# Banded attention with five key tiles: two turned tiles to ScalarE and three to VectorE, instead of one and four

## The chip, the core and the metric

One core of a Trainium2 chip runs the whole program. The metric is the device time in microseconds of one launch. The engines that matter here are TensorE (PE in the profile, its weight loads PEld), VectorE (DVE) and ScalarE (ACT); they run their own instruction streams and meet at semaphores.

## What is computed

A trunk of two layers over 2048 tokens of width 1024, in float32. Layer 0 runs a differential attention and a sliding-window attention; layer 1 projects its input and runs a chunked attention of 16 heads of 64, in which every chunk of 64 tokens attends to itself and the 8 chunks before it. Only the last is touched:

```
def one_chunk(args):
    qi, c = args
    start = c * CHUNK
    kb = lax.dynamic_slice_in_dim(kp, start, C_BAND, axis=2)
    vb = lax.dynamic_slice_in_dim(vp, start, C_BAND, axis=2)
    s = jnp.einsum('bhqd,bhkd->bhqk', qi, kb, preferred_element_type=jnp.float32) * ATTN_SCALE + bias
    s = jnp.where((start + koff) >= 0, s, -jnp.inf)
    p = jax.nn.softmax(s, axis=-1)
    return jnp.einsum('bhqk,bhkd->bhqd', p.astype(vb.dtype), vb)
```

## The kernel before

The program is a row of stages: project, diff_attn, band_attn (prefix b_), output, project, band_attn (prefix c_), output. The stages run one behind the other. band_attn is written once and used twice: with `back` = 1 (b_, a step is at most two key tiles wide) and with `back` = 4 (c_, up to five).

A step s of band_attn handles one tile of 128 queries (i = s % 16) of one pair of heads (hp = s // 16). Its `width(s)` is the number of key tiles of 128: 1, 2, 3, 4 in the first steps of a pair of heads, then 5 in the other twelve. With 16 heads there are 8 pairs and 128 steps, 96 of them five tiles wide, called full here. A step goes through these hands:

- qk(s), TensorE, line 1438: logits of both heads, into two accumulators of PSUM that every step uses again, so it waits for both maxima of step s-1.
- maximum(s, half), VectorE, line 1519: adds the bias, takes the row's extreme and writes to SBUF, one instruction and an accumulator read for each head.
- exponential(s, half), ScalarE, line 1550, in place, with the sum of the row.
- transposes(s), TensorE, line 1459: turns the 64-row halves of `prob` (chunk by chunk, `a`, tile by tile, `t`) into PSUM. The upper 64 rows and the lower 64 rows are worked off in pairs: while the upper half writes into its bank of `turned`, the lower one writes into another bank. Tiles from MAIN on, the far ones, go to the bank `turned_far`, which both halves use: the lower half does its far tiles first, the upper half last, and between them stands the semaphore `far_begun`.
- main_leaves(s), VectorE, line 1527: copies the tiles up to MAIN from `turned` to `prob_t` in SBUF.
- far_leaves(s), ScalarE, line 1563: copies the far tile from `turned_far`.
- pv(s), TensorE, line 1478: multiplies with the values; waits for both copies of step s.
- output_leaves, ScalarE, line 1557, every fourth step: copies the finished block out of PSUM.

The order on each engine is written out by hand. TensorE: qk(s), transposes(s-1), pv(s-2). VectorE: maximum(s, 0), maximum(s, 1), main_leaves(s-1). ScalarE: exponential(s, 0), exponential(s, 1), far_leaves(s-1), and every fourth step output_leaves. transposes(s) waits for the exponentials of s and, since `turned` and `turned_far` exist once, for both copies of step s-1. GpSimd only prepares biases and the output weights beside it, and SyncE issues the loads and stores.

Of the kernel before, what the change touches and what calls it, by code (L numbers as in the profile page):

```python
# [26 lines left out]
P = 128  # L27
# [3 lines left out]
BLK = 512  # L31
NBLK = SEQ // BLK
TPB = BLK // P
HD = 64
# [1201 lines left out]
def band_attn(nc, before, name, keep, scr, heads, back, q_row, k_row, group, v_dram, skew, o_row, sinks, w_dram, w_loaded, w_hi, w_lo, post, share, ready=None, ssq=None, rms=None):  # L1236
# [4 lines left out]
    with ExitStack() as ctx:  # L1241
# [4 lines left out]
        sums = post.sums  # L1246
        WIDE = (back + 1) * P
        SPARE = 1 if sinks else 0
        MAIN = 4
        bias = st.sb("bias", [P, 4, WIDE]) if ready is None else ready.bias  # L1250
        prob = st.sb("prob", [P, 4, WIDE + SPARE])
        prob_t = st.sb("prob_t", [P, 2, back + 1, 2, P])
# [4 lines left out]
        END = BLK + NEAR  # L1257
        turned = st.ps("turned", [P, 2, BLK])
        turned_far = st.ps("turned_far", [P, BLK])
        o_ps = st.ps("o", [P, BLK])  # L1260
        HALVES = 2
        HALF = SEQ // HALVES
# [8 lines left out]
        pair_turned, far_begun, main_copied, far_copied = (st.sem(x) for x in ("pair_turned", "far_begun", "main_copied", "far_copied"))  # L1271
# [12 lines left out]
        def k_set(hp):  # L1284
            return hp % 2 if group == 1 else 2 * hp // group

        def loads(hp):
            return (hp - own_from) // 2 + 1

        def width(s):  # L1290
            return min(s % TILES, back) + 1

        def full(s):
            return min(width(s), MAIN)

        fars = [sum(width(e) > MAIN for e in range(s)) for s in range(PAIRS + 1)]

# [115 lines left out]
        @block.tensor  # L1413
        def _(pe):
            def qk(s):
                hp, i = divmod(s, TILES)
                b, kb, w = hp % 2, k_set(hp), width(s)
                if ready is not None:
                    if s == 0:
                        pe.wait_ge(ready.loaded, ready.LOADED)  # L1420
                elif hp == 0:
                    for n, (lo, hi) in enumerate(FIRST):
                        if i == lo // P:
                            pe.wait_ge(first_loaded[n], 16 * (LOADS + 1))
                if hp >= own_from and i % (TILES // HALVES) == 0:
                    pe.wait_ge(pair_loaded[b][i // (TILES // HALVES)], 16 * LOADS * loads(hp))
                if ready is not None and hp == 2 and i == 0:
                    pe.wait_ge(ready.keys_loaded, ready.KEYS_LOADED)
                if s >= 1:
                    pe.wait_ge(max_done, 2 * s)  # L1430
                cuts = [(END - w * P, BLK, i - w + 1)] if w > 2 else []
                near = min(w, 2)
                cuts.append((END - near * P, END, i - near + 1))
                for lo, hi, tile in cuts:
                    for n, (x, y) in enumerate(((0, 0), (0, 1), (1, 0))):
                        for half in range(2):
                            rows = slice(half * HD, (half + 1) * HD)
                            last = nc.tensor.matmul(logits[half][:, lo:hi], q_sb[b][x][rows, i * P:(i + 1) * P],  # L1438
                                                    k_sb[kb][y][rows, tile * P:tile * P + hi - lo], start=n == 0, stop=n == 2)
                last.then_inc(qk_done, 1)  # L1440

            def transposes(s):
                if s >= 1:
                    pe.wait_ge(main_copied, s)
                    if fars[s] > fars[s - 1]:
                        pe.wait_ge(far_copied, fars[s])
                main = [[(a, t) for t in range(full(s))] for a in range(2)]
                far = [[(a, t) for t in range(MAIN, width(s))] for a in range(2)]
                upper, lower = main[0] + main[1] + far[0] + far[1], far[0] + far[1] + main[0] + main[1]
                pe.wait_ge(exp_done, 2 * s + (2 if far[0] else 1))  # L1450
                for n in range(len(upper)):
                    if n == full(s):
                        pe.wait_ge(exp_done, 2 * s + 2)
                    if far[0] and n == 2 * MAIN:
                        pe.wait_ge(far_begun, fars[s + 1])
                    for part, (a, t) in enumerate((upper[n], lower[n])):
                        rows = slice(part * HD, (part + 1) * HD)
                        to = turned[:, part, (2 * t + a) * HD:(2 * t + a + 1) * HD] if t < MAIN else turned_far[:, (2 * part + a) * HD:(2 * part + a + 1) * HD]
                        last = nc.tensor.transpose(to, prob[rows, (2 * s + a) % 4, t * P:(t + 1) * P], keep["ident"][rows, rows])  # L1459
                    if far[0] and n == 1:  # L1460
                        last.then_inc(far_begun, 1)
                last.then_inc(pair_turned, 1)

            def pv(s):
                hp, i = divmod(s, TILES)
                pe.wait_ge(main_copied, s + 1)
                if fars[s + 1] > fars[s]:
                    pe.wait_ge(far_copied, fars[s + 1])
                if s % GROUP == 0 and s >= GROUP:
                    pe.wait_ge(o_done, s // GROUP)  # L1470
                if ready is None and hp >= own_from and i % (TILES // HALVES) == 0:
                    pe.wait_ge(v_loaded[hp % 2][i // (TILES // HALVES)], 16 * loads(hp))
                at = s % GROUP * P
                w = width(s)
                for t in range(w):
                    for half in range(2):
                        v = v_sb[:, hp % 2, half, i - w + 1 + t, :] if ready is None else v_sb[:, k_set(hp), i - w + 1 + t, :]
                        last = nc.tensor.matmul(o_ps[half * HD:(half + 1) * HD, at:at + P], v,  # L1478
                                                prob_t[:, s % 2, t, half, :], start=t == 0, stop=t == w - 1)
                last.then_inc(pv_done, 1)  # L1480

            if sinks:
                pe.wait_ge(zero_set, len(logits))
            for s in range(PAIRS + 2):
                if s < PAIRS:
                    qk(s)
                if 1 <= s <= PAIRS:
                    transposes(s - 1)
                if s >= 2:
                    pv(s - 2)  # L1490
# [52 lines left out]
        @block.scalar  # L1543
        def _(act):
            def exponential(s, half):
                hp, i = divmod(s, TILES)
                j = (2 * s + half) % 4
                act.wait_ge(max_done, 2 * s + half + 1)
                p = prob[:, j, 0:width(s) * P + SPARE]
                nc.scalar.activation(p, p, ACT.Exp, bias=neg_max[:, j:j + 1], scale=-1.0,  # L1550
                                     accum_out=sums[:, 2 * hp + half, i:i + 1]).then_inc(exp_done, 1)

            def output_leaves(n):
                act.wait_ge(pv_done, (n + 1) * GROUP)
                if n >= 2:
                    act.wait_ge(stored[n % 2], 16 * (n // 2))
                nc.scalar.activation(o_out[:, n % 2, :], o_ps[:, :], ACT.Copy).then_inc(o_done, 1)

            def far_leaves(s):
                act.wait_ge(pair_turned, s + 1)  # L1560
                if s >= 2:
                    act.wait_ge(pv_done, s - 1)
                nc.scalar.copy(prob_t[:, s % 2, MAIN, :, :].rearrange("p a (r q) -> p r a q", r=2),
                               turned_far[:, 0:2 * P].rearrange("p (r a q) -> p r a q", r=2, a=2)).then_inc(far_copied, 1)

            if ready is None:
                for n in range(len(FIRST)):
                    first_piece(act, n, 1)
            for s in range(PAIRS + 2):
                if s < PAIRS:  # L1570
                    exponential(s, 0)
                    exponential(s, 1)
                if 1 <= s <= PAIRS and width(s - 1) > MAIN:
                    far_leaves(s - 1)
                if s == PAIRS and ssq is not None:
                    act.wait_ge(mean_done, 1)
                    nc.scalar.activation(root[:, :, :], mean[:, :, :], ACT.Sqrt).then_inc(root_done, 1)
                if s >= 2 and (s - 2) % GROUP == GROUP - 1:
                    output_leaves((s - 2) // GROUP)
# [248 lines left out]
```

## Time and profile before

| | us |
|---|---|
| median of 3 runs | 2651.3 (2649.97 to 2653.81) |
| the profiled execution | 2649.35 |
| its span, first to last instruction | 2647.5 |
| TensorE busy in the span | 2384.7 (90%) |
| VectorE busy | 1473.0 (56%) |
| ScalarE busy | 1161.6 (44%) |
| GpSimd busy | 1132.2 (43%) |

The page of the profile gives busy shares over the whole span, which holds seven stages with different limits; the stage at hand takes about 390 us of it, from 2046 to 2440 us. It has to be read from the timeline of its own steps. In the rows below, times are microseconds from the span's start; in brackets stands how long the engine had been idle and what ended most of it. The timeline merges neighbouring instructions of a kind into one row with a count. The ends of matmuls are modelled.

### The profile page before, as it was taken

The page shows a single profiled execution, that of the slowest core. Times are in us where ns is not written, and L with a number is a line of the kernel's source. Part 1 is how long each engine was busy: PE and PEld are TensorE (multiplying, and loading weights), DVE is VectorE, ACT ScalarE, POOL GpSimd, SP SyncE. Part 2 cuts the span into 40 slices and gives each one's busy share as a digit, 9 for nine tenths or more (in the row PEclk, how much of TensorE's full clock was granted, in tenths as well). Part 3 has the DMA queues.
Part 4 walks back from the last instruction along what each step waited for, and adds up shares of the span by engine and source line. Part 5 has one row for each costly group of instructions (what it writes and reads, how often), then busy time and mean ns, then how long its engine had stood idle before and what let it go on. Part 6 is the DMA issues. An engine that isn't in the chain of part 4 may idle for free. (4 is left out here: it accounts for less than half of the span.)

```text
span 2647.5 us, 44254 instructions
## 1 busy us (share of the span) xinstructions
PE 2384.7 (90%) x16760; PEld 1996.6 (75%) x16760; DVE 1473.0 (56%) x2823; ACT 1161.6 (44%) x2484; POOL 1132.2 (43%) x892
## 2 busy tenths in 40 slices
PE   2999979996899998989959999799997899998998
PEld 2877868875778876668848888688886778887887
DVE  4344445334887795755634422544323778887565
ACT  5333343333777775722133333433332666665211
POOL 5887878771000002311058887888874201100000
PEclk7999989998999999989979999899999999999999
DMA  3455434457563133565534443434433453453352
GB/s 103 151 191 183 140 118 149 149 172 153 118 140 92 45 120 89 167 216 207 199 109 154 164 130 100 155 125 170 131 100 108 167 192 122 145 173 113 138 212 80
DMA packets 220882, 376.63 MB, mean 142 GB/s; under 512 B 54996, under 2 KB 109440, under 8 KB 219648
## 3 DMA queue, kind: packets, MB, share of 16 engines
q1 hardware_dynamic: 199280, 297.78, 35.2%
q0 software_dynamic: 18992, 72.36, 9.2%
q10 hardware_dynamic: 2400, 3.67, 0.5%
q8 instruction: 135, 2.21, 0.3%
q14 instruction: 75, 0.61, 0.1%
HBM read 236.33 MB, written 142.90 MB: 143 GB/s over the span
## 5 line engine op out<-in xcount | busy, mean ns | idle before, releaser
L808 PE MATMUL p_acc<-p_a_hi,p_w_hi 128*128 128x512 f32 x1624 | 643.4, 396 | 37.0 <-DVE p_a_lo L593 33.5
L808 PE MATMUL p_acc<-p_a_hi,p_w_lo 128*128 128x512 f32 x1624 | 636.8, 392 | 0.0
L808 PE MATMUL p_acc<-p_a_lo,p_w_hi 128*128 128x512 f32 x1624 | 636.1, 392 | 0.0
L236 POOL TENSOR_TENSOR p_w_lo<-p_w_raw,p_w_hi 128x512 fp32r<-128x512 f32 x252 | 350.6, 1401 | 121.0 <-ACT p_w_hi L474 120.5
L808 PEld LDWEIGHTS p_acc<-p_a_hi,p_w_hi 128*128 128x128 f32 x1624 | 307.6, 189 | 106.1 <-DVE p_a_lo L593 34.6
L808 PEld LDWEIGHTS p_acc<-p_a_hi,p_w_lo 128*128 128x128 f32 x1624 | 307.1, 189 | 65.5
L808 PEld LDWEIGHTS p_acc<-p_a_lo,p_w_hi 128*128 128x128 f32 x1624 | 307.7, 189 | 62.3
L474 ACT ACTIVATE p_w_hi<-p_w_raw 128x512 fp32r<-128x512 f32 x252 | 156.7, 623 | 268.6 <-POOL p_w_raw L254 110.3
L1550 ACT ACTIVATE c_prob<-c_prob,c_neg_max 128x640 f32<-128x640 f32 (+4 forms) x256 | 193.2, 755 | 142.4 <-DVE c_neg_max L1519 141.9
L667 DVE SCALAR_TENSOR_TENSOR p_lo_out<-p_full_out,p_hi_out 128x512 fp32r<-128x512 f32 x116 | 125.0, 1078 | 208.1 <-ACT p_hi_out L488 208.1
L1519 DVE CUSTOM_DVE_ANT_0 c_prob<-c_logits,c_bias 128x640 f32<-128x640 f32 (+4 forms) x256 | 179.5, 738 | 81.0 <-PE c_logits L1438 61.7
L1744 PE MATMUL o_acc<-w_out_hi,o_m_hi 128*128 128x512 f32 x512 | 203.7, 398 | 4.8 <-DVE o_m_lo L1696 4.8
L1744 PE MATMUL o_acc<-w_out_hi,o_m_lo 128*128 128x512 f32 x512 | 201.0, 393 | 0.0
L1744 PE MATMUL o_acc<-w_out_lo,o_m_hi 128*128 128x512 f32 x512 | 200.9, 392 | 0.0
L1103 ACT ACTIVATE a_prob<-a_prob,a_neg_max 128x128 f32<-128x128 f32 (+15 forms) x128 | 153.5, 1199 | 47.2 <-DVE a_neg_max L1063 46.4
L1438 PE MATMUL c_logits<-share 64*128 64x256 f32 (+2 forms) x1440 | 138.2, 322 | 33.2 <-DVE c_neg_max L1519 16.1
L696 DVE COPY p_full_out<-p_acc 128x512 f32<-128x512 f32 x58 | 40.1, 691 | 216.3 <-PE p_acc L808 216.2
L1438 PEld LDWEIGHTS c_logits<-share 64*128 64x128 f32 x1440 | 111.9, 188 | 58.1 <-DVE c_neg_max L1519 27.9
L1478 PE MATMUL c_o<-c_prob_t,c_v 128*64 128x128 f32 x2240 | 151.6, 279 | 1.6 <-issue 1.6
L236 POOL TENSOR_TENSOR p_w_lo<-ready_w,p_w_hi 128x512 fp32r<-128x512 f32 x96 | 132.3, 1388 | 36.8 <-ACT p_w_hi L474 36.4
L1527 DVE COPY c_prob_t<-c_turned 128x1024 f32<-128x1024 f32 (+3 forms) x128 | 143.3, 1120 | 6.1 <-PE c_turned L1459 6.1
L474 ACT ACTIVATE p_w_hi<-p_t 128x512 fp32r<-128x512 f32 x58 | 36.6, 632 | 239.9 <-issue 122.5
(192 smaller groups left out, 4338.0 us busy)
## 6 DMA issues: line engine op xcount, KB each, us to landing
scr_qh<-p_hi_out SPq DMA_DIRECT2D x116, 256.0 KB, 2.4
scr_ql<-p_lo_out SPq DMA_DIRECT2D x116, 256.0 KB, 2.6
p_w_raw<-in_w_in_even POOLq DMA_DIRECT2D x26, 1024.0 KB, 7.6
scr_gt<-p_hi_out SPq DMA_DIRECT2D x128, 128.0 KB, 2.0
ready_w<-in_w_in_odd POOLq DMA_DIRECT2D x16, 1024.0 KB, 7.7
p_w_raw<-in_w_in_odd POOLq DMA_DIRECT2D x16, 1024.0 KB, 7.5
share<-scr_qh SPq DMA_DIRECT2D x28, 512.0 KB, 9.3
share<-scr_ql SPq DMA_DIRECT2D x28, 512.0 KB, 10.4
```

The lines of the kernel that those rows point to most:

```text
L236: nc.gpsimd.tensor_tensor(w_lo[:, k, :, :], w_source(e, k), w_hi[:, k, :, :].bitcast(F32), ALU.subtract).then_inc(w_made, 1)
L474: nc.scalar.activation(w_hi[:, k, :, :], w_source(e, k), ACT.Copy).then_inc(w_cast, 1)
L667: nc.vector.scalar_tensor_tensor(out=lo_out[:, buf, :], in0=full_out[:, buf, :], scalar=factor, in1=hi_out[:, buf, :].bitcast(F32), op0=AL ...
L696: nc.vector.tensor_copy(full_out[:, n % 2, :], x[:, :]).then_inc(taken, 1)
L808: last = nc.tensor.matmul(bank[:, :], wt[:, k, c, :], at[:, k, c, :], start=starts and step == 0, stop=step == 3 * HK - 1, skip_group_chec ...
L1103: nc.scalar.activation(p, p, ACT.Exp, bias=neg_max[:, j:j + 1], scale=-1.0, accum_out=row_sum[:, g % 2, m:m + 1]).then_inc(exp_done, 1)
L1438: last = nc.tensor.matmul(logits[half][:, lo:hi], q_sb[b][x][rows, i * P:(i + 1) * P], k_sb[kb][y][rows, tile * P:tile * P + hi - lo], sta ...
L1478: last = nc.tensor.matmul(o_ps[half * HD:(half + 1) * HD, at:at + P], v, prob_t[:, s % 2, t, half, :], start=t == 0, stop=t == w - 1)
L1519: nc.vector.tensor_tensor_reduce(out=prob[:, j, 0:n + SPARE], in0=logits[half][:, END - n:END + SPARE], in1=bias[:, b, WIDE - n:WIDE + SPARE],
L1527: nc.vector.tensor_copy(prob_t[:, s % 2, 0:n, :, :].rearrange("p t a (r q) -> p r (t a) q", r=2), turned[:, :, 0:n * P].rearrange("p r (x ...
L1550: nc.scalar.activation(p, p, ACT.Exp, bias=neg_max[:, j:j + 1], scale=-1.0, accum_out=sums[:, 2 * hp + half, i:i + 1]).then_inc(exp_done, 1)
L1744: last = nc.tensor.matmul(acc[u % 4][:, :], mt[:, t % 2, c, :], wt[:, c, half * BLK:(half + 1) * BLK], start=step == 0, stop=step == 3 * K ...
```

## The change

MAIN goes from 4 to 3. VectorE copies the first three key tiles of a step and ScalarE the tiles from the fourth on: two in a five-tile step and one in a four-tile step, where before it had none. In `turned_far` the lower half's tiles now begin at the middle of the bank (FAR), and ScalarE's copy takes both. The lower half turns all its far tiles first, four transposes in a full step where there were two, and signals `far_begun` behind the last of them, the 8th transpose of the step instead of the 4th; the upper half waits for it ahead of its own far tiles, which are now its last four instead of its last two: ahead of the 13th transpose instead of the 17th. The b_ stage, with at most two tiles, issues the same instructions as before.

```diff
--- before.py
+++ after.py
@@ -1246,7 +1246,7 @@
         sums = post.sums
         WIDE = (back + 1) * P
         SPARE = 1 if sinks else 0
-        MAIN = 4
+        MAIN = 3
         bias = st.sb("bias", [P, 4, WIDE]) if ready is None else ready.bias
         prob = st.sb("prob", [P, 4, WIDE + SPARE])
         prob_t = st.sb("prob_t", [P, 2, back + 1, 2, P])
@@ -1257,6 +1257,7 @@
         END = BLK + NEAR
         turned = st.ps("turned", [P, 2, BLK])
         turned_far = st.ps("turned_far", [P, BLK])
+        FAR = BLK // 2
         o_ps = st.ps("o", [P, BLK])
         HALVES = 2
         HALF = SEQ // HALVES
@@ -1455,9 +1456,9 @@
                         pe.wait_ge(far_begun, fars[s + 1])
                     for part, (a, t) in enumerate((upper[n], lower[n])):
                         rows = slice(part * HD, (part + 1) * HD)
-                        to = turned[:, part, (2 * t + a) * HD:(2 * t + a + 1) * HD] if t < MAIN else turned_far[:, (2 * part + a) * HD:(2 * part + a + 1) * HD]
+                        to = turned[:, part, (2 * t + a) * HD:(2 * t + a + 1) * HD] if t < MAIN else turned_far[:, FAR * part + (2 * (t - MAIN) + a) * HD:FAR * part + (2 * (t - MAIN) + a + 1) * HD]
                         last = nc.tensor.transpose(to, prob[rows, (2 * s + a) % 4, t * P:(t + 1) * P], keep["ident"][rows, rows])
-                    if far[0] and n == 1:
+                    if far[0] and n == 2 * len(far[0]) - 1:
                         last.then_inc(far_begun, 1)
                 last.then_inc(pair_turned, 1)
 
@@ -1560,8 +1561,9 @@
                 act.wait_ge(pair_turned, s + 1)
                 if s >= 2:
                     act.wait_ge(pv_done, s - 1)
-                nc.scalar.copy(prob_t[:, s % 2, MAIN, :, :].rearrange("p a (r q) -> p r a q", r=2),
-                               turned_far[:, 0:2 * P].rearrange("p (r a q) -> p r a q", r=2, a=2)).then_inc(far_copied, 1)
+                n = width(s) - MAIN
+                nc.scalar.copy(prob_t[:, s % 2, MAIN:MAIN + n, :, :].rearrange("p t a (r q) -> p r (t a) q", r=2),
+                               turned_far[:, :].rearrange("p (r x q) -> p r x q", r=2, q=HD)[:, :, 0:2 * n, :]).then_inc(far_copied, 1)
 
             if ready is None:
                 for n in range(len(FIRST)):
```

## Rows read from the trace of the kernel before

**Rows 1.** Stretches of c_: length, busy PE, PEld, DVE, ACT, POOL, clock, DMA share, GB/s

```profile
2046.00:2092.00 46.00, 36.66 (x546) 31.99 (x548) 29.92 (x65) 24.66 (x63) 9.03 (x8) 0.82 0.68 259
2092.00:2440.00 348.00, 322.03 (x5381) 282.02 (x5377) 285.21 (x577) 222.80 (x578) 31.61 (x31) 1.00 0.44 140
```

**Rows 2.** Timeline of TensorE over two full steps: start, duration (us), line, operation, count

```profile
2078.11 1.16 PE L1438 MATMUL c_logits<-share 64*128 64x384 f32 x12
2079.13 0.24 PE L1459 MATMUL c_turned<-keep_ident,c_prob 64*128 64x64 f32 x1
...
2079.89 1.31 PE L1478 MATMUL c_o<-c_prob_t,c_v 128*64 128x128 f32 x20
2081.13 1.16 PE L1438 MATMUL c_logits<-share 64*128 64x384 f32 x12
2082.37 0.24 PE L1459 MATMUL c_turned<-keep_ident,c_prob 64*128 64x64 f32 x1
...
2082.49 0.22 PE L1459 MATMUL c_turned_far<-keep_ident,c_prob 64*128 64x64 f32 x1
...
2082.89 0.22 PE L1459 MATMUL c_turned_far<-keep_ident,c_prob 64*128 64x64 f32 x1
...
2084.38 1.16 PE L1438 MATMUL c_logits<-share 64*128 64x384 f32 x12
```

**Rows 3.** Timeline of VectorE, same steps

```profile
2079.41 0.82 DVE L1519 CUSTOM_DVE_ANT_0 c_prob<-c_logits,c_bias 128x640 f32<-128x640 f32 x1 [0.53 <-PE c_logits L1438]
...
2080.91 1.22 DVE L1527 COPY c_prob_t<-c_turned 128x1024 f32<-128x1024 f32 x1
2082.44 0.82 DVE L1519 CUSTOM_DVE_ANT_0 c_prob<-c_logits,c_bias 128x640 f32<-128x640 f32 x1 [0.31 <-PE c_logits L1438]
```

**Rows 4.** Timeline of ScalarE, same steps

```profile
2081.11 0.82 ACT L1550 ACTIVATE c_prob<-c_prob,c_neg_max 128x640 f32<-128x640 f32 x1
...
2081.93 0.35 ACT L1563 COPY c_prob_t<-c_turned_far 128x256 f32<-128x256 f32 x1
```

**Rows 5.** Waits in the steady stretch: who waited for whom, us in total, times, longest

```profile
PEld c_turned L1459 <- DVE c_prob_t L1527: 18.2, 50, 1.4
...
PE c_turned L1459 <- ACT c_prob_t L1563: 7.7, 21, 1.2
```

**Rows 6.** Groups by shape in one head pair: count, busy us, mean ns, idle before

```profile
L1550 ACT ACTIVATE c_prob<-c_prob,c_neg_max 128x640 f32<-128x640 f32 x24 | 19.7, 822 | 12.4 <-DVE c_neg_max L1519 12.4
...
L1527 DVE COPY c_prob_t<-c_turned 128x1024 f32<-128x1024 f32 x13 | 15.9, 1220 | 0.7 <-PE c_turned L1459 0.7
...
L1563 ACT COPY c_prob_t<-c_turned_far 128x256 f32<-128x256 f32 x12 | 4.2, 351 | 0.0
...
L1557 ACT ACTIVATE c_o_out<-c_o 128x512 f32<-128x512 f32 x4 | 2.4, 588 | 0.0
L1550 ACT ACTIVATE c_prob<-c_prob,c_neg_max 128x512 f32<-128x512 f32 x3 | 2.2, 718 | 2.1 <-DVE c_neg_max L1519 2.1
L1527 DVE COPY c_prob_t<-c_turned 128x768 f32<-128x768 f32 x2 | 1.9, 952 | 0.0
```

**Rows 7.** Timeline of all engines at the first full step of a head pair

```profile
2258.59 1.22 DVE L1527 COPY c_prob_t<-c_turned 128x1024 f32<-128x1024 f32 x1
...
2259.52 0.18 ACT L1550 ACTIVATION_READ_ACCUMULATOR c_prob<-c_prob,c_neg_max 128x1 f32 x1
...
2259.87 0.27 PE L1459 MATMUL c_turned<-keep_ident,c_prob 64*128 64x64 f32 x1
```

**Rows 8.** Timeline of TensorE from the pair's last full step to the next pair

```profile
2294.34 0.24 PE L1459 MATMUL c_turned<-keep_ident,c_prob 64*128 64x64 f32 x1 [0.67 <-ACT c_prob_t L1563]
...
2300.47 0.98 PE L1438 MATMUL c_logits<-share 64*128 64x256 f32 x12 [0.64 <-DVE c_neg_max L1519]
```

**Rows 9.** Busy time by engine in 80 us inside the b_ stage (1040 to 1120)

```profile
sum 80.00, PE 74.28 PEld 55.99 DVE 63.66 ACT 56.37 POOL 29.23; mean PE 37.14 PEld 28.00 DVE 31.83 ACT 28.18 POOL 14.61
```

**Rows 10.** Timeline of TensorE at one of the stops without a releaser

```profile
2129.50 0.76 PE L1478 MATMUL c_o<-c_prob_t,c_v 128*64 128x128 f32 x9 [1.55 <-issue]
```

## The prediction

> **What bounds the kernel now.** I first looked at the whole span (2647.5 us, profiled execution 2649.35 us, median of the runs 2651.3 us) and asked where tiles beyond the third exist. Only the second banded attention (prefix c_) has steps wider than two tiles; the first (b_) has at most two, so nothing of it is touched. The c_ stage runs from about 2046 to 2440 us. In its steady stretch TensorE is busy 322.0 of 348.0 us, VectorE 285.2, ScalarE 222.8, at full clock [rows 1]. Shares alone suggest that VectorE is the fuller of the two copying engines and that TensorE is nearly full. Neither says which wait ends last, so I next read the timeline of two full (five-tile) steps.
>
> TensorE's order is qk(s), transposes(s-1), pv(s-2). In one step nothing is missing: qk starts at 2078.11, transposes at 2079.13, pv at 2079.89, the next qk at 2081.13 [rows 2]. So a full step is 3.02 us of TensorE work: 1.02 + 0.76 + 1.24. The next step is not back to back: qk starts at 2081.13, its transposes only at 2082.37, 1.24 instead of 1.02 us later; the next qk at 2084.38 [rows 2]. So steps alternate 3.02 and 3.25 us, mean 3.13. Over a whole head pair it is the same: transposes of the first full step start at 2259.87, those of the last at 2294.34, 34.47 us for 11 steps, 3.13 each [rows 7, 8].
>
> Who holds the transposes back? They need three things: the exponentials of their own step, VectorE's copy of the previous step, and ScalarE's copy of the previous step. VectorE's copy is over at 2080.91 + 1.22 = 2082.13, 0.24 us before the transposes [rows 3]. ScalarE's copy starts when the second exponential lets it, at 2081.93, lasts 0.35, ends at 2082.28, and the transposes start 0.09 later [rows 4, 2]. **ScalarE's copy is last, by 0.15 us.** The table of waits puts most of this idle time down to VectorE's copy (18.2 us, 50 times) and less to ScalarE's (7.7 us, 21 times) [rows 5]; such a wait is for several semaphores, and the clock times decide.
>
> That gives a loop. From the start of qk(s) to the start of transposes(s) there is one chain: qk ends, first maximum at 2079.41, first and behind it second exponential, the latter at 2081.11, far copy 2081.93, transposes 2082.37 [rows 2 to 4]; in all 2082.37 - 2078.11 = 4.26 us, call it L. The transposes (0.77) and the pv behind them (1.24) must pass before qk(s+2). Two steps therefore take L + 0.77 + 1.24 = 6.27 us, 3.135 per step, which is what the trace shows. VectorE is not in this loop after its second maximum, and waits 0.31 to 0.53 us for logits in every step [rows 3].
>
> **The change part by part.** (1) VectorE's copy goes from 128x1024 (1220 ns) to 128x768 (952 ns), 0.27 us less [rows 6]. It was 0.15 us from being last and gets further from it. Worth nothing in the loop; 0.27 us only if it were last.
>
> (2) ScalarE's copy goes from 128x256 (351 ns) to 128x512. The nearest row is ScalarE's other copy out of PSUM of just that size, 588 ns [rows 6]: +0.24 us. Bounds: the slope of the exponentials, (822 - 718) ns for 128 elements [rows 6], would give 0.21 for 256 more; twice the whole instruction gives 0.35. I take 0.24. It stands in L with nothing beside it: the exponentials before it are back to back, the transposes are waiting. Below nothing isn't possible, for the same instruction moves twice the data. The Trainium skill ("ScalarE: Activation LUTs", section "Step-by-step: what each stage is for") gives 0.833 ns per element, which would make it 0.213 us and the total below 17.3 instead of 18.7; no row times the strided copy at this size.
>
> (3) The transposes. Their number is the same (20 per full step). Before, the signal that the lower half's far tiles are through (far_begun) hangs on the 4th transpose and is waited for ahead of the 17th. Now it hangs on the 8th and is waited for ahead of the 13th. The 1st transpose starts at 2082.37 and the 17th at 2082.89, so they start 0.0325 us apart, and one lasts 0.22 [rows 2]. The 8th starts at about 2082.60 and ends at 2082.82; with the 0.09 us that a release took above, the 13th could start at 2082.91, where it stood at about 2082.76: a gap of 0.15 us. By the same working the old wait was met at 2082.49 + 0.22 + 0.09 = 2082.80, ahead of 2082.89, and indeed there is no gap in the trace. Bounds: 0 (the signal is seen before the matmul's modelled end) and 0.20 (the signal takes the 0.14 us that VectorE's maximum starts behind the end of qk: 2078.11 + 1.16 = 2079.27 to 2079.41 [rows 2, 3]). I take 0.15. Nothing hides it: what is behind it on TensorE is pv and the next qk, and both are in the loop. It does not occur in a four-tile step, where the signal hangs on the 4th transpose.
>
> (4) Four-tile steps (8 in all, one per head pair) now have a far copy (one tile, 0.35) and wait for both exponentials. In that step the second exponential ends before TensorE comes to it, so nothing is lost there. But the transposes of the first full step, which started at 2259.87 just behind VectorE's copy (2258.59 + 1.22), now wait for ScalarE: read of the accumulator from 2259.52, far copy about 2259.61 to 2259.96, transposes 2260.06: +0.19 [rows 7]. No DMA, queue or other wait is moved.
>
> **The sum.** Per head pair: the first full step's transposes +0.19, the second's +0.24. From there each round of two steps costs 0.24 + 0.15 = 0.39 more; the last (twelfth) full step is five rounds behind the second: 0.24 + 5 x 0.39 = 2.19, and its own gap makes 2.34. TensorE's work alone would be 3.02 + 0.15 = 3.17 us, below the loop's 3.33 per step, so the loop stays the bound. The narrow steps after it hang on that point: transposes of the last full step at 2294.34, pv, qk, and then each qk behind the maxima before it (idle 0.64 <-DVE at 2300.47) [rows 8], with no slack to swallow anything. 8 x 2.34 = 18.7 us. The output stage starts when this one ends, with its weights long there, so all of it reaches the end: 2649.35 + 18.7 = 2668.1 for the profiled execution, and from the median, which lies 1.95 higher, 2651.3 + 18.7 = 2670.0.
>
> In the same way the bounds: 0.21 and no gap gives 0.21 + 5 x 0.21 = 1.26 per pair, 10 us, 2661; 0.35 and a gap of 0.20 gives 0.35 + 5 x 0.55 + 0.20 = 3.30, 26 us, 2678.
>
> **Rivals.** A (forecast): ScalarE's copy is last, and both the copy and the gap cost. 2670, in its bounds 2661 to 2678; chance 0.85, of which some 0.2 for the copy alone (0.24 x 6 x 8 = 11.5, so 2663).
>
> B, the other side: VectorE's copy is what releases the transposes, as the table of waits says [rows 5], and ScalarE has room (222.8 busy of 348.0 [rows 1]). With 0.27 us less on VectorE the loop would shorten until TensorE's own 3.02 us bound it: at most 0.11 us for each of 96 full steps, 10.6 us, so 2641. It decides if two things hold at once: the release by VectorE's copy takes 0.24 us, and ScalarE's copy at 128x512 costs hardly more than 0.35, most of it being fixed. Against the first, where VectorE's copy alone is waited for, the transposes start 0.06 behind its end (2258.59 + 1.22 = 2259.81, 2259.87 [rows 7]); against the second, the 588 ns of its neighbour. Chance 0.05. The Trainium skill would have it so ("TensorEngine Tiling (Array Packing)", section "PSUM Bottleneck"): use both ScalarE and VectorE to empty PSUM. Both are used already, and [rows 2 to 4] show the one that gets more work to be the later one; the rule counts work and not the order on an engine.
>
> C, no difference: the hidden slack is larger than I read (the ends of matmuls are modelled), and copy and gap fall into the idle 0.22 us that every second step has. 2651, or within 5; chance 0.06.
>
> D, more than A: TensorE's pauses grow and its clock falls to the lower level in parts of the stage. The b_ stage is at full clock with TensorE busy 74.3 of 80.0 us [rows 9]; here it would be about 88%, which no row shows. In the first stretch of c_, with a mean clock of 0.82 of full, TensorE was busy 36.7 of 46.0 us [rows 1]. A few such stretches would give 2690 or more; chance 0.04.
>
> A few steps have a stop of TensorE that no semaphore explains (1.55 us of "issue" at 2129.50 [rows 10]). The number of instructions hardly changes, so I count them as equal, but they may fall elsewhere: 2 to 3 us on either side, for which the range's lower end is taken at 2658 instead of 2661; the upper end, by the same allowance, at 2680. This leaves out B, C and D. Taking 0.2% (5.3 us) as about what a measurement of this kernel can tell from no change: faster 0.05 (B), within 0.06 (C), slower 0.89 (A and D).
>
> **What would show it.** ScalarE's far copy at 128x512 in 0.56 to 0.63 us; VectorE's at 128x768 in 0.95, with its wait for logits longer, not shorter; transposes 0.09 us behind the end of the far copy; a gap of about 0.15 us between the 12th and 13th transpose; full steps of 3.33 us on average; a c_ stage 18.7 us longer and all other stages alike. It would be wrong if the gap in the transposes weren't there (2663), or if in a full step the transposes started behind VectorE's copy (B), or if the mean step stayed 3.13 although the copy got longer (C).

## Result and profile after

| | before | after |
|---|---|---|
| median, 5 runs each | 2649.97 us | 2665.58 us |
| ratio, 95% interval | | 1.0059 (1.0045 to 1.0073) |
| profiled execution | 2649.35 | 2663.84 |
| c_ stage, first qk to last pv | 2048.2 to 2439.3, 391.1 | 2047.1 to 2453.1, 406.0 |
| an undisturbed pair of heads (the fifth; from the start of qk of its first full step to that of the next pair's) | 2255.80 to 2302.97, 47.17 | 2261.32 to 2310.63, 49.31 |
| VectorE busy, whole span | 1473.0 | 1446.2 |
| ScalarE busy, whole span | 1161.6 | 1184.3 |

The changed kernel is slower by 15.6 us, and the trace puts it in the c_ stage: that stage is 14.9 us longer there, the whole profiled execution 14.5.

The groups by shape in the fifth head pair of the changed kernel (window 2261.32 to 2310.63) answer to [rows 6]:

```profile
L1528 DVE COPY c_prob_t<-c_turned 128x768 f32<-128x768 f32 x15 | 14.3, 953 | 1.0 <-PE c_turned L1460 1.0
L1565 ACT COPY c_prob_t<-c_turned_far 128x512 f32<-128x512 f32 x12 | 6.8, 566 | 0.3 <-PE c_turned L1460 0.3
```

VectorE's copy lost 0.27 us, ScalarE's gained 0.215: together less work than before. The steady stretch, by engine, answers to [rows 1]:

```profile
2092.00:2453.00 361.00, 339.21 (x5398) 290.20 (x5396) 260.38 (x578) 243.59 (x587) 31.40 (x30) 1.00 0.42 135
```

VectorE and ScalarE are now nearly even (260.4 and 243.6 of 361.0 us), and it took longer. Two full steps of the changed kernel, TensorE first, answer to [rows 2]:

```profile
2281.99 0.24 PE L1460 MATMUL c_turned<-keep_ident,c_prob 64*128 64x64 f32 x1
...
2282.23 0.22 PE L1460 MATMUL c_turned_far<-keep_ident,c_prob 64*128 64x64 f32 x1
2282.26 0.31 PE L1460 MATMUL c_turned<-keep_ident,c_prob 64*128 64x64 f32 x4
2282.51 0.27 PE L1460 MATMUL c_turned_far<-keep_ident,c_prob 64*128 64x64 f32 x1
...
2282.90 1.31 PE L1479 MATMUL c_o<-c_prob_t,c_v 128*64 128x128 f32 x20
2284.14 1.14 PE L1439 MATMUL c_logits<-share 64*128 64x384 f32 x12
2285.22 0.24 PE L1460 MATMUL c_turned<-keep_ident,c_prob 64*128 64x64 f32 x1
...
2286.14 1.31 PE L1479 MATMUL c_o<-c_prob_t,c_v 128*64 128x128 f32 x20
2287.38 1.14 PE L1439 MATMUL c_logits<-share 64*128 64x384 f32 x12
2288.61 0.24 PE L1460 MATMUL c_turned<-keep_ident,c_prob 64*128 64x64 f32 x1
```

The 9th to the 12th transpose start from 2282.26 on, 0.03 us apart, the last at about 2282.35; the 13th (the `c_turned_far` row at 2282.51) starts 0.16 us later: the gap. From transposes to pv it is 0.91 us (2281.99 to 2282.90; 2285.22 to 2286.14 is 0.92), before 0.76 to 0.77. Steps take 3.23 and 3.39 us, 3.31 on average. VectorE and ScalarE in the same step, as in [rows 3, 4]:

```profile
2282.05 0.82 DVE L1520 CUSTOM_DVE_ANT_0 c_prob<-c_logits,c_bias 128x640 f32<-128x640 f32 x1 [0.79 <-PE c_logits L1439]
...
2283.55 0.95 DVE L1528 COPY c_prob_t<-c_turned 128x768 f32<-128x768 f32 x1
2285.44 0.82 DVE L1520 CUSTOM_DVE_ANT_0 c_prob<-c_logits,c_bias 128x640 f32<-128x640 f32 x1 [0.94 <-PE c_logits L1439]
```

```profile
2283.75 0.81 ACT L1551 ACTIVATE c_prob<-c_prob,c_neg_max 128x640 f32<-128x640 f32 x1
...
2284.56 0.56 ACT L1565 COPY c_prob_t<-c_turned_far 128x512 f32<-128x512 f32 x1
```

VectorE's copy ends at 2284.50, before ScalarE's even starts. ScalarE's ends at 2285.12, the transposes start at 2285.22. VectorE now waits 0.79 to 0.94 us for logits where it waited 0.31 to 0.53.

The table of waits in the steady stretch (2092 to 2456) answers to [rows 5]:

```profile
PEld c_turned L1460 <- issue: 12.7, 45, 0.6
...
PE c_turned L1460 <- ACT c_prob_t L1565: 7.1, 16, 1.1
...
PEld c_turned L1460 <- DVE c_prob_t L1528: 5.9, 7, 1.3
```

What stood under VectorE's copy before (18.2 us, 50 times) mostly stands under "issue" now that VectorE's copy ends 0.7 us before the transposes. ScalarE's row hardly moves, though by the clock times it is ScalarE that is waited for in both kernels. The rows of PEld and PE aren't different stops: PEld is TensorE's weight load and PE the matmul behind it, and they tell of one stop twice. The stop of [rows 8] (PE at 2294.34, 0.67 us, put down to ScalarE) stands in the trace of before for the weight load as

```profile
2294.31 0.14 PEld L1459 LDWEIGHTS c_turned<-keep_ident,c_prob 64*128 64x128 f32 x1 [0.79 <-DVE c_prob_t L1527]
```

VectorE's copy had ended at 2294.10 there, ScalarE's at 2294.24. Taken step by step, ScalarE's copy was the last of the two in 43 of the 50 waits that the PEld row of before puts down to VectorE (16.8 of its 18.2 us), and the PE row, all ScalarE, was right.

### The profile page after: what moved, and what is told of

The parts are those of the page before. It is cut to its first block and busy times, and to the rows that moved or that the text cites. A ratio compares the mean times of both kernels' runs of the same rounds, so it can differ in the third digit from the quotient of the medians.

```text
span 2662.0 us, 44278 instructions
## 1 busy us (share of the span) xinstructions
PE 2401.6 (90%) x16760; PEld 2004.2 (75%) x16760; DVE 1446.2 (54%) x2823; ACT 1184.3 (44%) x2492; POOL 1132.2 (43%) x892
## 5 line engine op out<-in xcount | busy, mean ns | idle before, releaser
L1479 PEld LDWEIGHTS c_o<-c_prob_t,c_v 128*64 128x64 f32 x2240 | 120.2, 137 | 9.5 <-issue 0.8
```

## Experiments

The theory: two steps take L (from qk(s) through the first maximum, the exponentials and ScalarE's copy to transposes(s)) plus transposes plus pv; the change lengthens the copy in L and the transposes by a gap. The rivals: VectorE's copy is what releases the transposes (B); copy and gap vanish in TensorE's idle time (C). The fifth head pair tells them apart best, since nothing disturbs it; its two times are the starts of the qk of its first full step and of the next pair's. Beside the first four kernels the kernel before had a median of 2651.39 us (20 runs), beside the last three, on another chip, 2652.70 (8 runs).

| kernel | fifth head pair, us | against 47.17 | median of its runs in us, ratio to before (95% interval) |
|---|---|---|---|
| gap only | 2259.11 to 2307.16: 48.05 | +0.88 | 2656.49, 1.002 (1.0011 to 1.003) |
| copy only | 2260.85 to 2309.29: 48.44 | +1.27 | 2660.95, 1.0037 (1.0023 to 1.0051) |
| VectorE's copy short | 2257.88 to 2305.13: 47.25 | +0.08 | 2652.14, 1.0006 (0.9997 to 1.0015) |
| copy first | 2247.75 to 2293.89: 46.14 | -1.03 | 2641.78, 0.9962 (0.9947 to 0.9976) |
| copy first, changed kernel | 2268.02 to 2318.09: 50.07 | +2.90 | 2672.93, 1.0071 (1.0056 to 1.0086) |
| changed kernel again | 2264.49 to 2313.82: 49.33 | +2.16 | 2666.58, 1.0047 (1.0033 to 1.0062) |
| signal behind the 8th | 2256.43 to 2303.73: 47.30 | +0.13 | 2649.89, one run |

**The gap alone.**

```diff
-                    if far[0] and n == 1:
+                    if far[0] and n == 5:
                         last.then_inc(far_begun, 1)
```

> The kernel before with one thing changed: far_begun is signalled behind the 12th transpose of a full step instead of the 4th, the wait stays ahead of the 17th, so the distance is that of the changed kernel (8th to 13th) and the copies stay 128x1024 and 128x256. Theory A (the loop qk, maximum, exponentials, ScalarE's copy, transposes, pv sets the step and the gap lies in it): a gap of 0.15 us in every full step, two steps of 6.27 become 6.42, a head pair 5 x 0.15 + 0.15 = 0.9 us longer (47.17 to 48.1), 7 us in all. Rival C (the gap falls into idle time of TensorE): the gap is seen, but the head pair stays at 47.2 and the time within 2 us of before.

Measured: +0.88 us per head pair, against 0.9 by theory A and none by C. The time is 5.1 us above the median of before, and not 7 (on the stops that make up such differences between traces see "The size" below: here they are 0.8 us, in the trace of before 4.5). TensorE in one full step:

```profile
2279.12 0.24 PE L1459 MATMUL c_turned<-keep_ident,c_prob 64*128 64x64 f32 x1
...
2279.76 0.27 PE L1459 MATMUL c_turned_far<-keep_ident,c_prob 64*128 64x64 f32 x1
...
2280.03 1.31 PE L1478 MATMUL c_o<-c_prob_t,c_v 128*64 128x128 f32 x20
```

The 17th transpose, first of the last row of them, starts 0.64 us behind the 1st, where [rows 2] have 0.52 (2082.37 to 2082.89), and pv comes 0.91 behind the first transpose instead of the 0.76 of [rows 2]. The 0.15 us are in the loop, and for the gap C falls. All twelve full steps have the gap (1.8 us together) and half of it shows: one step in two has TensorE idle ahead of its transposes anyway, and there a gap in the step before costs nothing.

**The copy alone.**

```diff
-        prob_t = st.sb("prob_t", [P, 2, back + 1, 2, P])
+        prob_t = st.sb("prob_t", [P, 2, back + 2, 2, P])
...
-                nc.scalar.copy(prob_t[:, s % 2, MAIN, :, :].rearrange("p a (r q) -> p r a q", r=2),
-                               turned_far[:, 0:2 * P].rearrange("p (r a q) -> p r a q", r=2, a=2)).then_inc(far_copied, 1)
+                nc.scalar.copy(prob_t[:, s % 2, MAIN:MAIN + 2, :, :].rearrange("p t a (r q) -> p t r a q", r=2),
+                               turned_far[:, 0:2 * P].rearrange("p (t r a q) -> p t r a q", t=1, r=2, a=2).to_broadcast([P, 2, 2, 2, HD])).then_inc(far_copied, 1)
```

> The kernel before, with ScalarE's far copy made 128x512 by writing the same tile to two places (the second is a spare tile that nothing reads); VectorE's copy and the transposes as before. Theory A: the copy takes 0.566 instead of 0.351 us, all of the 0.215 is in the loop: a head pair 6 x 0.215 = 1.3 us longer, 10.3 us in all; with the gap of the other experiment it should add up to the changed kernel's 2.14 us per head pair. Rival B (VectorE's copy releases the transposes): ScalarE's copy would have to pass 0.15 us of room first, at most 6 x 0.065 = 0.4 us per pair, 3 us in all.

Measured: the copy takes 565 ns, the head pair is 1.27 us longer (theory A 1.3, B at most 0.4), the time 9.6 us. Here too six of the twelve copies count. ScalarE, and TensorE behind it:

```profile
2280.57 0.56 ACT L1563 COPY c_prob_t<-c_turned_far 128x512 f32<-128x512 f32 x1
```

```profile
2279.78 1.14 PE L1438 MATMUL c_logits<-share 64*128 64x384 f32 x12
2281.23 0.24 PE L1459 MATMUL c_turned<-keep_ident,c_prob 64*128 64x64 f32 x1 [0.31 <-ACT c_prob_t L1563]
...
2282.00 1.31 PE L1478 MATMUL c_o<-c_prob_t,c_v 128*64 128x128 f32 x20
```

The copy ends at 2281.13, the transposes start 0.10 later. Gap and copy together, 0.88 + 1.27 = 2.15 us, are the changed kernel's 2.14, with VectorE's copy at its old length in both. So the 0.27 us taken from VectorE, over 12 full steps of a head pair, gave back nothing that shows.

**VectorE's copy short, nothing else.** The kernel leaves the fourth tile out: it is not copied, and its place holds zeros that are set once.

```diff
-                n = full(s)
+                n = min(full(s), 3)
...
+            if not sinks:
+                nc.vector.memset(prob_t[:, :, 3, :, :], 0.0).then_inc(zero_set, 1)
+                dve.wait_ge(zero_set, 1)
             for s in range(PAIRS + 1):
```

> The kernel before, with VectorE copying only three of the four tiles of turned (128x768, 0.95 us); the fourth is left out, its place in prob_t is zeroed once, so that tile takes no part in the output. ScalarE's copy and the transposes as before. Theory A: VectorE's copy is not last, nothing changes in a full step: head pair 47.2 us (at most 0.05 less from the first full step, which waits for VectorE), time within 1 us of before. Rival B: the step shrinks until TensorE's 3.02 us bind, up to 1.3 us per head pair and 10 us in all.

Measured: head pair 47.25 us, time 0.8 us above before with an interval that holds 1. B falls directly: the part of the change that was to relieve the fuller engine is worth nothing in this order of work. VectorE and TensorE in one step:

```profile
2276.16 0.95 DVE L1527 COPY c_prob_t<-c_turned 128x768 f32<-128x768 f32 x1
2277.69 0.82 DVE L1519 CUSTOM_DVE_ANT_0 c_prob<-c_logits,c_bias 128x640 f32<-128x640 f32 x1 [0.58 <-PE c_logits L1438]
```

```profile
2276.38 1.16 PE L1438 MATMUL c_logits<-share 64*128 64x384 f32 x12
2277.62 0.24 PE L1459 MATMUL c_turned<-keep_ident,c_prob 64*128 64x64 f32 x1
```

The copy is over at 2277.11, and the transposes still start 1.24 us behind qk, as in [rows 2]. What VectorE saves it waits.

**ScalarE's copy first.** If the copy behind the exponentials is what is late, its place matters more than its size.

```diff
+                if 1 <= s <= PAIRS and width(s - 1) > MAIN:
+                    far_leaves(s - 1)
                 if s < PAIRS:
                     exponential(s, 0)
                     exponential(s, 1)
-                if 1 <= s <= PAIRS and width(s - 1) > MAIN:
-                    far_leaves(s - 1)
```

> The kernel before, with ScalarE's order turned: far_leaves(s-1) ahead of exponential(s, 0) and (s, 1) instead of behind them. Theory A: the copy leaves the chain between the second exponential and the transposes; then VectorE's copy (0.15 us earlier) is last, L falls from 4.26 to about 4.12, two steps from 6.27 to 6.13, a step from 3.135 to 3.06: 0.9 us less per head pair, 7 us in all, the transposes now 0.06 to 0.1 behind the end of VectorE's copy. Rival (the copy ahead of the first exponential only moves the delay: it waits for the transposes and pushes the exponential by 0.2 us in each step): a step at 3.13 or more, time as before or longer.

Measured: 46.14 us per head pair, steps of 3.04, and 2641.78 us, faster than before (0.9962) and some 24 us below the changed kernel. It is more than was expected (0.9 us per pair, 7 us in all); the pair accounts for 8 x 1.03 = 8.2 of the 9.6 us. ScalarE, VectorE and TensorE in two steps:

```profile
2261.80 0.37 ACT L1563 COPY c_prob_t<-c_turned_far 128x256 f32<-128x256 f32 x1 [1.05 <-PE c_turned L1459]
2262.06 0.83 ACT L1550 ACTIVATE c_prob<-c_prob,c_neg_max 128x640 f32<-128x640 f32 x1
```

```profile
2259.64 1.22 DVE L1527 COPY c_prob_t<-c_turned 128x1024 f32<-128x1024 f32 x1
...
2262.67 1.22 DVE L1527 COPY c_prob_t<-c_turned 128x1024 f32<-128x1024 f32 x1
```

```profile
2259.87 1.16 PE L1438 MATMUL c_logits<-share 64*128 64x384 f32 x12
2260.92 0.27 PE L1459 MATMUL c_turned<-keep_ident,c_prob 64*128 64x64 f32 x1
...
2261.68 1.31 PE L1478 MATMUL c_o<-c_prob_t,c_v 128*64 128x128 f32 x20
2262.92 1.15 PE L1438 MATMUL c_logits<-share 64*128 64x384 f32 x12
2263.95 0.27 PE L1459 MATMUL c_turned<-keep_ident,c_prob 64*128 64x64 f32 x1
```

The copy sits in the time in which ScalarE used to wait for the maximum. VectorE's copies end at 2260.86 and 2263.89, and both times the transposes start 0.06 later, the release that [rows 7] show where VectorE's copy alone is waited for. From qk to transposes it is now 4.08 us (2259.87 to 2263.95), and 4.08 + 0.76 + 1.24 is 6.08, 3.04 per step. VectorE's copy is last here, but it costs next to nothing: where nothing is missing TensorE starts its transposes 1.02 us behind the start of a qk [rows 2], and here it starts them 1.03 to 1.05 behind.

**The same on the changed kernel.** The edit is the same.

> The changed kernel (three tiles on VectorE, two on ScalarE) with ScalarE's order turned as in the experiment before: far_leaves(s-1) ahead of the exponentials. If the copy first simply helps, it saves here what it saved there (1.0 us per head pair), and the time falls to about 2656. If ScalarE's work is now in a loop of one step (transposes(s-1), copy, two exponentials, transposes(s)), a step is 0.98 (transposes with their gap) + 0.04 + 0.48 (the copy of 0.57 until the next instruction starts) + 0.83 + 0.82 + 0.20 (release) = 3.35 us against 3.31 in the changed kernel: nothing saved, a head pair 49.3 to 49.9 us, the time 2665 to 2670. The second is what I expect.

Measured: 50.07 us per head pair, full steps of 3.38 to 3.39, 2672.93 us: 6 us slower than the changed kernel beside it, and above what was expected (49.3 to 49.9, 2665 to 2670), though by the loop that was expected. What saved 1.03 us per pair there costs 0.7 here. ScalarE and TensorE:

```profile
2283.24 0.59 ACT L1565 COPY c_prob_t<-c_turned_far 128x512 f32<-128x512 f32 x1 [1.17 <-PE c_turned L1460]
2283.72 0.83 ACT L1551 ACTIVATE c_prob<-c_prob,c_neg_max 128x640 f32<-128x640 f32 x1
...
2284.55 0.82 ACT L1551 ACTIVATE c_prob<-c_prob,c_neg_max 128x640 f32<-128x640 f32 x1
...
2286.62 0.59 ACT L1565 COPY c_prob_t<-c_turned_far 128x512 f32<-128x512 f32 x1 [1.17 <-PE c_turned L1460]
```

```profile
2285.60 0.24 PE L1460 MATMUL c_turned<-keep_ident,c_prob 64*128 64x64 f32 x1
```

Now the loop has one step: the copy waits for the transposes, both exponentials wait for the copy, the next transposes for the exponentials. 0.48 + 0.83 + 1.05 (2284.55 to the transposes at 2285.60) + 1.02 (from there to the next copy, the transposes with their gap) = 3.38. The gap and the longer copy count once in every step here, not once in two.

**The changed kernel again**, beside the others on one chip:

> The changed kernel itself, beside the others on the same chip: 0.59% above the kernel before, 2665 to 2667 us, a head pair 49.3 us.

Measured: 49.33 us per head pair and 13.9 us above before, with an interval (1.0033 to 1.0062) that overlaps the first.

**How near may the signal be?**

```diff
-                    if far[0] and n == 1:
+                    if far[0] and n == 3:
                         last.then_inc(far_begun, 1)
```

> The kernel before with far_begun signalled behind the 8th transpose instead of the 4th, the wait ahead of the 17th as before: 9 transposes between signal and wait, where the kernel before has 13 and the changed one 5. If the gap is the signal's way (about 0.30 us from the start of the transpose that signals to the weight load that waits) less the transposes in between (0.031 us each), it is 0 to 0.03 us here and a head pair stays at 47.2 to 47.4 us. If any wait so near costs its 0.15 us, a head pair is 48.05 us.

Measured: 47.30 us per head pair, 0.13 more than before. TensorE in one full step:

```profile
2276.20 0.24 PE L1459 MATMUL c_turned<-keep_ident,c_prob 64*128 64x64 f32 x1
...
2276.73 0.27 PE L1459 MATMUL c_turned_far<-keep_ident,c_prob 64*128 64x64 f32 x1
...
2276.99 0.55 PE L1478 MATMUL c_o<-c_prob_t,c_v 128*64 128x128 f32 x6
```

The 17th transpose, at 2276.73, is hardly late (0.53 us behind the first, before 0.52); from first transpose to pv it is 0.79 us, 0.02 more than before. So with signal and wait 13 transposes apart nothing is lost, 9 apart some 0.02 us, 5 apart 0.15: about the signal's way less the transposes that lie in it. The gap is no fixed price of a wait.

## Why the prediction was right

**The loop.** Forecast: steps of 3.33 us, the transposes 0.09 us behind ScalarE's copy, a gap ahead of the 13th transpose, VectorE waiting longer. Measured: 3.31, 0.10, 0.15, 0.79 to 0.94. The two experiments that did one half of the change each gave +0.88 and +1.27 us per head pair, and the one that only relieved VectorE gave nothing. The loop adds up in the changed kernel as it did before: from qk to transposes 4.47 us (2284.14 is a qk, its own transposes start at 2288.61), transposes to pv 0.91, pv to qk 1.24, together 6.62 for two steps. The step that decided the sign was to take the end of each copy from the timeline, against the PEld row of the table of waits. That the table put less of the idle time down to ScalarE was misread, though: its two rows are the same stops, and the PE row had the releaser right.

That nothing hides the gap was too strong, and the sum didn't go by it: it counts gap and copy once in two steps, and the two experiments show just that (0.88 for twelve gaps of 0.15, 1.27 for twelve copies longer by 0.215).

**The size.** 18.7 us were forecast, 15.6 and 13.9 measured in two sets of runs. Two terms of the sum were off. ScalarE's copy was sized by its neighbour of the same shape, 588 ns, and took 566: +0.215 instead of +0.24, which makes 0.215 + 5 x (0.215 + 0.15) + 0.15 = 2.19 per head pair instead of 2.34; measured 2.14, 17.1 us for eight. The measured slope is (566 - 351) / 256 = 0.84 ns per element. The figure of the Trainium skill ("ScalarE: Activation LUTs", section "Step-by-step: what each stage is for"), 0.833 ns per element, agrees with it and was nearer than the row that I took; the sum by it is 17.4, not the 17.3 of the prediction. The second term is the stops without a releaser, counted as equal in both kernels. They weren't in the two traces. In the trace of before the second, third and fourth steps from pair to pair took 49.07, 48.73 and 48.18 us instead of 47.17, 4.5 us of such stops; in the changed kernel the second and third took 50.32 and 49.85 instead of 49.3, 1.6 us. Its first took 50.14, and that isn't a stop: the first full step's qk ran at the lower clock still (0.50 of full until 2064.2, in the trace of before until 2062.7, just as that qk began) and took

```profile
2061.74 1.97 PE L1439 MATMUL c_logits<-share 64*128 64x384 f32 x12
```

instead of 1.16, which cost 0.8 us. The three together are the difference between 8 x 2.14 = 17.1 and the stage's 14.9: without them the stage is 386.6 us before and 403.6 after, 17.0 longer. How much a kernel has of them can't be told from one trace: the changed kernel, traced again, had 0.9 us of stops instead of 1.6 and hardly anything from the clock (its c_ stage 404.7 us, 403.8 without the stops). Nor do the stops lie elsewhere in every kernel: in all nine traces each one of over 0.3 us on TensorE's matmuls in this stage comes in one of three turns of TensorE, those that begin with the qk of step 25, 42 or 58 counted from 0 (that of [rows 10] in the first of them), at the same places in the program and not at the same times. What they are isn't settled. The medians, 15.6 and 13.9 apart, are also below 17.1; whether the stops make that isn't shown, for one execution of each kernel was profiled. The range had 2 to 3 us for them.

The gap's size came out partly by luck. The forecast took 0.22 + 0.09 = 0.31 us from the start of the signalling transpose to that of the waiting one, and it is 0.28: the 13th transpose is 0.13 us late (0.16 behind the 12th instead of 0.03). The last 0.02 us are lost behind it, in the last transposes, and bring the step to the 0.15 of the forecast.

**Rivals.** B fell by the copy made short and, the other way round, by the copy put first: only there is VectorE's copy last in the steady steps. C fell by the gap alone and by the copy alone, each of which costs what one step in two can't hide. D did not come: the steady stretch kept its full clock with TensorE busy 339.2 of 361.0 us, 94%. The 88% that I had expected was wrong; before it was 93% [rows 1]. The share rose because the gap is counted as busy: the 12th transpose's modelled 0.22 us reach past the start of the 13th, 0.16 us behind it. In the fifth head pair TensorE was busy 44.3 us before and also with the copy alone, 45.7 with the gap alone and 46.5 in the changed kernel; that the last is higher still isn't explained by it. The upper bounds (0.35 for the copy, 0.20 for the gap) were too wide.

**The four-tile step.** It now waits for a far copy. The first full step's transposes were forecast 0.19 us later; in the changed kernel they start 4.26 us behind their qk (2261.32 to 2265.58), before 4.07 (2255.80 to 2259.87, the latter in [rows 7]): 0.19.

The separation of signal and wait comes from the layout: "TensorEngine Tiling (Array Packing)" of the Trainium skill, section "Gotcha 1: PSUM Pressure", has it that different row tiles can't access one bank at the same time and that software must see to it. No run here shows what happens without the wait; it wasn't tried.

## What to carry to other kernels

In a loop of waits like this one, moving work from the fuller engine to the emptier one helps only if the fuller one ends the wait; add up the loop from clock times (here qk, maximum, two exponentials, copy, transposes, pv, for two steps) and see which copy ends last. Before its size, look at the place of the late instruction in its engine's order: put ahead of the exponentials, into time in which ScalarE waited, the small copy gave 9.6 us; the same move with the larger copy closed a new loop of one step and cost 6. TensorE's semaphore to itself was free only with enough other work between signal and wait, here some ten transposes.

## What the runs showed of the hardware

The way of a semaphore from a transpose back to a wait on TensorE itself takes 0.28 us, from the start of the transpose that signals to the start of the one that waits (2282.23 to 2282.51 in the changed kernel). Transposes start 0.031 us apart, so some 9 or 10 of them cover it (13 apart lost nothing, 9 apart about 0.02 us, 5 apart 0.15).

A wait on two semaphores can be put down to the wrong one in most steps of a stage: weight loads whose wait ScalarE's copy ended stood under VectorE's copy (43 of 50 times) while that one ended 0.15 us earlier, and under "issue" (12.7 us) once it ended 0.6 us earlier than ScalarE's. The row of the matmul behind such a weight load had the right one.
